# Start and end of a two-layer decoder trunk: other load order, other place for the semaphore starts, a shorter last Newton chain, and a shared last scaling

## The chip, the cores and the metric

The kernel runs on one core of a Trainium2 chip. The metric is device time in microseconds (us) of one execution, as the median of several. The program is one launch; all weights and inputs are in HBM at its start, and the output is in HBM at its end.

## The reference

Two layers over x (1 x 512 x 1024, f32), with 256 memory tokens:

```python
for i in range(DEPTH):                       # DEPTH = 2
    h = rms_norm(x, attn_norm_w[i])
    proj = h @ w_in[i]                       # q, k, v, latents, xq and the gates
    y_a = (differential attention) @ w_o_diff[i]
    y_b = (latent attention) @ w_o_mla[i]
    mh = rms_norm(mem, mem_norm_w[i])
    y_c = (cross attention into mh @ w_mem_kv[i]) @ w_o_cross[i]
    x = x + (g_a * y_a + g_b * y_b + g_c * y_c) @ w_out[i]
    h2 = rms_norm(x, ffn_norm_w[i])
    f_gate, f_up = split(h2 @ w_gate_up[i])
    x = x + (silu(f_gate) * f_up) @ w_down[i]
return rms_norm(x, final_norm_w)
```

with `rms_norm(x, w) = x * rsqrt(mean(x*x) + 1e-6) * w`. The rope tables come from cos and sin of `positions`.

## The kernel before

It is written engine by engine, with semaphores by hand; each engine runs its own list in the order in which it stands, so the order of the code is the order of the work.

**Tiling.** x is kept transposed: xT has 8 tiles (`KD`) of 128 channels by 512 tokens. A weight column block of 128 (a "slot") is 8 tiles of 128 x 128. To multiply f32 at f32r speed, each operand is split in a high and a low part, and a product is three matmuls (L602 to L604, in `unit`): high by high, low by high, high by low. 512 columns are one matmul.

**A slot's way.** SyncE loads it in two DMAs into one of two `raw` buffers (L434, in `slot`), after `slot_lo` says that the buffer is free again. ScalarE copies it to `w_hi` (L1109; for the first four slots by `first_slot`, L1367). GpSimd subtracts to get `w_lo` (L564). Then TensorE may use it. There are four w_hi/w_lo pairs. `slot_lo` starts at 2 by two small memsets of GpSimd (L536).

**The start (layer 0).** x comes in four column quarters of 512 KB (`load_x`, L422; semaphores in_x0 to in_x3), laid out with tokens on the partitions. After seven small matmuls on the identity (L874), TensorE transposes x tile by tile (`flip_x`, L876 to L882, four 128 x 128 transposes a tile, two tiles a quarter) into seven PSUM banks. ScalarE turns a tile into `h_hi`, times the gain (`first_tile`, L1372), VectorE makes `h_lo` (L1977). The first two slots of layer 0, here called N0 (cross query) and N1 (a gate), are multiplied by h tile by tile; N0 waits for each h_lo tile (`tile_split`, L889). Before N0 six tiles are transposed, and tiles 6 and 7 stand between N0's second and third tile. After N1 come the transposes of the memory tokens (L910), which wait for `mem_scaled`; then six of the eight tiles of slot N2; then the column sums of squares of x (L614), which wait for `x_sum` (`sq_added`); then the rest. x_sum is built by ScalarE's squares (L1403, four of 128 x 1024) and VectorE's adds (L1989, three, and L1990). The squares stand behind the memory's squares (L1389), a copy of slot N2, an activation table load (L1394) and the memory's 1/rms (L1397, L1399). A second table, that of Sin (loaded at L1374), serves sin_t and half_t (L1385, L1386), which wait for VectorE's angles (L1960 to L1973, from `pos_i`).

**Semaphore starts.** Each engine begins with `start_counts` (L406): one semaphore increment for each counter that it drives: 9 for TensorE (L576), 35 for VectorE (L1639) and 37 for ScalarE (L1106).

**The end.** The last tile of the down projection is done in two halves of 256 tokens (`last_down`, L1052). Behind each half VectorE adds it to xT (L2215), makes the gained copy (L2218), ScalarE squares (L1622), VectorE adds into x_sum (L2220), TensorE transposes (L1073) and sums over the channels (L1083, result `ssq`), ScalarE takes Ln and Exp (L1626, L1628), VectorE refines in `newton` (four operations, L1781 to L1784, 128 x 2). Then each half has two blocks of 128 tokens by 1024 to scale and store: the even one by VectorE (L2225), stored by SyncE (L521), and the odd one by ScalarE (L1631), stored from ScalarE's queue (L1633).

## Time and profile before

| | |
|---|---|
| median of 3 runs | 1964.63 us (1964.38 to 1966.5) |
| the profiled execution, its own time | 1964.07 us |
| its span, first to last instruction | 1961.9 us |
| TensorE busy | 1947.8 us (99%) |
| VectorE, ScalarE, GpSimd busy | 1037.2, 935.8, 1074.4 us |
| the chain that ended last | TensorE 98%, GpSimd 1% |
| TensorE's mean granted clock | 0.999 |

"Busy" adds up the time in which an engine had an instruction under way. The chain that ended last is followed back from the last instruction, at each step to whatever released it. A kernel whose chain is TensorE at 98% can gain without fewer matmuls only where TensorE stands idle: here 14.1 us of the span.

### The profile page before, as it was taken

How to read it: one execution, taken by the hardware profiler on the slowest of the kernel's cores; microseconds unless marked ns; L12 is line 12 of the kernel's file. 1: busy time of each engine (PE TensorE's matmuls, PEld its weight loads, DVE VectorE, ACT ScalarE, POOL GpSimd, SP SyncE). 2: the span in 40 equal slices, each digit the busy share in tenths (PEclk: the TensorE clock that was granted, in tenths of full speed). 3: DMA queues.
4: the chain of work that ended last, by engine and by line, in shares of the span. 5: the costliest groups of instructions: out<-in, count | busy, mean ns of one | idle time of the engine just before them, and what ended most of it. 6: DMA issues, size and time to landing. Idle time of an engine off the chain costs nothing.

```text
span 1961.9 us, 28882 instructions
## 1 busy us (share of the span) xinstructions
PE 1947.8 (99%) x9340; PEld 1632.6 (83%) x9340; DVE 1037.2 (53%) x1900; ACT 935.8 (48%) x1665; POOL 1074.4 (55%) x1422
## 2 busy tenths in 40 slices
PE   8999999999999999999999999999999999999998
PEld 7888888888888888888888888888888888888887
DVE  6445888887655333321144658888876443333111
ACT  6444666776544322233344456776674342222332
POOL 6654454445554555557765645344445555555674
PEclk9999999999999999999999999999999999999999
DMA  6443233224543333333344323223356333333232
GB/s 195 128 148 92 76 91 87 81 76 140 183 145 96 102 95 98 94 115 89 109 138 120 111 85 92 81 76 89 90 158 191 113 99 94 98 96 96 84 92 91
DMA packets 356001, 212.61 MB, mean 108 GB/s; under 512 B 14274, under 2 KB 339906, under 8 KB 355396
## 3 DMA queue, kind: packets, MB, share of 16 engines
q1 hardware_dynamic: 338288, 173.32, 30.7%
q10 hardware_dynamic: 17620, 38.07, 5.5%
q8 instruction: 56, 0.92, 0.2%
q14 instruction: 37, 0.30, 0.0%
HBM read 190.88 MB, written 20.45 MB: 108 GB/s over the span
## 4 chain that ended last, share of the span: by engine, by line
PE 98%; POOL 1%; DVE 0%; issue 0%; DMA 0%; ACT 0%; SPq 0%; POOLq 0%
PE proj L602 24%; PE proj L604 24%; PE proj L603 24%; PE score L602 2%; PE score L603 2%; PE score L604 2%; PE flip L656 2%; PE score L638 2%; PE score L816 1%; PE score L818 1%; PE score L642 1%; PE score L641 1%; PE att L583 1%; PE att L584 1%; PE att L582 1%; PE score L830 1%
## 5 line engine op out<-in xcount | busy, mean ns | idle before, releaser
L564 POOL TENSOR_TENSOR w_lo<-raw,w_hi 128x256 fp32r<-128x256 f32 x1376 | 1069.3, 809 | 866.1 <-ACT w_hi L1109 864.9
L602 PE MATMUL proj<-h_hi,w_hi 128*128 128x512 f32 x1584 | 626.3, 395 | 0.6 <-DVE h_lo L1977 0.3
L604 PE MATMUL proj<-h_hi,w_lo 128*128 128x512 f32 x1584 | 618.1, 390 | 0.0
L603 PE MATMUL proj<-h_lo,w_hi 128*128 128x512 f32 x1584 | 616.9, 389 | 0.0
L1109 ACT ACTIVATE w_hi<-raw 128x1024 fp32r<-128x1024 f32 x344 | 362.5, 1055 | 195.4 <-PE proj L604 55.2
L604 PEld LDWEIGHTS proj<-h_hi,w_lo 128*128 128x128 f32 x1584 | 297.3, 188 | 63.3
L602 PEld LDWEIGHTS proj<-h_hi,w_hi 128*128 128x128 f32 x1584 | 297.6, 188 | 60.6 <-issue 0.9
L603 PEld LDWEIGHTS proj<-h_lo,w_hi 128*128 128x128 f32 x1584 | 297.7, 188 | 58.9 <-issue 0.2
L602 PE MATMUL proj<-hid_hi,w_hi 128*128 128x512 f32 x330 | 129.0, 391 | 0.0
L604 PE MATMUL proj<-hid_hi,w_lo 128*128 128x512 f32 x330 | 128.5, 389 | 0.0
L603 PE MATMUL proj<-hid_lo,w_hi 128*128 128x512 f32 x330 | 128.4, 389 | 0.0
L1580 ACT ACTIVATE sig_f<-gate_n 128x512 f32<-128x512 f32 x44 | 27.8, 632 | 163.1 <-DVE gate_n L2176 163.1
L1109 ACT ACTIVATE hid_hi<-hid 128x512 f32 (+1 forms) x44 | 27.8, 633 | 160.8 <-DVE hid L2183 160.8
L2176 DVE TENSOR_TENSOR gate_n<-proj,rstd 128x512 f32<-128x512 f32 x44 | 30.3, 688 | 129.7 <-PE proj L604 129.7
L1109 ACT ACTIVATE pt_hi<-flip 128x384 fp32r<-128x384 f32 (+1 forms) x112 | 55.4, 532 | 89.1 <-PE flip L656 88.8
L1722 DVE TENSOR_TENSOR pt_lo<-flip,pt_hi 128x384 fp32r<-128x384 f32 (+1 forms) x112 | 64.7, 607 | 62.1 <-ACT pt_hi L1109 62.1
L2183 DVE TENSOR_TENSOR hid<-proj,gated 128x512 f32<-128x512 f32 x44 | 30.4, 691 | 106.1 <-PE proj L604 106.0
L1942 DVE TENSOR_TENSOR xT<-xT,proj 128x512 f32 x24 | 16.5, 687 | 120.3 <-PE proj L604 120.3
L604 PEld LDWEIGHTS proj<-hid_hi,w_lo 128*128 128x128 f32 x330 | 61.9, 188 | 12.9
L603 PEld LDWEIGHTS proj<-hid_lo,w_hi 128*128 128x128 f32 x330 | 62.0, 188 | 12.7
L602 PEld LDWEIGHTS proj<-hid_hi,w_hi 128*128 128x128 f32 x330 | 62.0, 188 | 12.7
L602 PE MATMUL score<-outs_hi,w_hi 128*128 128x512 f32 x160 | 62.3, 390 | 0.0
(420 smaller groups left out, 3147.2 us busy)
## 6 DMA issues: line engine op xcount, KB each, us to landing
raw<-in_w_in SPq DMA_DIRECT2D x224, 256.0 KB, 3.1
raw<-in_w_gate_up SPq DMA_DIRECT2D x176, 256.0 KB, 3.0
raw<-in_w_down SPq DMA_DIRECT2D x96, 192.0 KB, 2.5
gate_in<-gate_scratch ACTq DMA_DIRECT2D x48, 256.0 KB, 4.1
gate_scratch<-gate_out ACTq DMA_DIRECT2D x46, 256.0 KB, 2.0
raw<-in_w_mem_kv SPq DMA_DIRECT2D x32, 256.0 KB, 2.9
raw<-in_w_o_diff SPq DMA_DIRECT2D x32, 256.0 KB, 2.9
raw<-in_w_out SPq DMA_DIRECT2D x32, 256.0 KB, 2.9
```

What stands on the lines that cost most here:

```text
L564: ins = g.tensor_tensor(w_lo[s][:, cols], raw[s % 2][:, cols], w_hi[s][:, cols].bitcast(F32), ALU.subtract)
L582: mm(o, sh, mh, start=n == 0, stop=False)
L602: mm(o, hi[:, c:c + width], rh, start=start and k == 0, stop=False)
L603: mm(o, hi[:, c:c + width], rl, start=False, stop=False)
L604: ins = mm(o, lo[:, c:c + width], rh, start=False, stop=stop and k == n - 1)
L638: ins = mm(o, mqT[0:96, cols], mkT[0:96, 0:(t + 1) * P], start=t != 0, stop=t == group[-1])
L656: ins = nc.tensor.transpose(b[:, col:col + P], p[:, q_off(t) + j * P:q_off(t) + (j + 1) * P], ident[:, :])
L1109: return sc.activation(out, in_, ACT.Copy)
L1580: sc.activation(sig_f[:, e, :], gate_n[:, :], ACT.Sigmoid).then_inc(silu_sig.sem, 1)
L1722: v.tensor_tensor(dst, src, hi.bitcast(F32), ALU.subtract).then_inc(flip_read.sem, 1)
L2176: v.tensor_tensor(gate_n[:, :], proj[0][:, :], rstd[:, :], ALU.mult).then_inc(gate_read.sem, 1)
L2183: v.tensor_tensor(hid[:, e, :], proj[1][:, :], gated[:, :], ALU.mult).then_inc(hid_ready.sem, 1)
```

## The change

Seven edits, six of them in the start and the end:

- SyncE: slot N0's weights are loaded first, then quarters 0 and 1 of x, slot N1's weights, quarters 2 and 3, the memory.
- TensorE: the transposes of tiles 4, 5 stand before N0's third tile and those of 6, 7 before its fifth; four tiles are transposed ahead of N0.
- ScalarE's 37 semaphore starts are issued by TensorE, behind its seven small matmuls. ScalarE issues the DMA of the positions before that of the gains.
- ScalarE takes the two Sin behind its second tile of h, and its copy of slot N2 behind the memory's 1/rms.
- Last norm: VectorE forms w0 = -(ssq + eps)/2 when ssq has been read by Ln (beside Exp), and then r*r, times w0, and (that + 1.5) * r: three operations behind Exp, where four were.
- The last odd block: ScalarE scales 768 columns, VectorE 256, ahead of its own even block.
- ScalarE's store waits for VectorE's counter too, SyncE's second store for its third count, TensorE's last sums for `half_shifted` where they waited for `y_rstd`.

```diff
+SHARE = 768
@@ sync
-            load_x(0)
-
                 slot(l, "N", 0, 0, *whole(w_in, l, C_XQ))
                 if l == 0:
-                    for quarter in range(1, 4):
-                        load_x(quarter)
+                    load_x(0)
+                    load_x(1)
                 slot(l, "N", 0, 1, *gate(l, GATES_N))
                 if l == 0:
+                    load_x(2)
+                    load_x(3)
                     sp.dma_start(mem_in[:, :, :], mem[0, :, :].rearrange("(t p) d -> p t d", p=P)).then_inc(in_mem, 16)
@@
-                sp.wait_ge(y_scaled[0], n + 1)
+                sp.wait_ge(y_scaled[0], 2 * n + 1)
@@ tensor
+            start_counts(pe, "act")
@@
-            for k in range(KD - 2):
+            for k in range(KD // 2):
                 flip_x(k)
@@
-                    if l == 0 and k == 2:
-                        flip_x(KD - 2)
-                        flip_x(KD - 1)
+                    if l == 0 and k in (2, 4):
+                        flip_x(k + 2)
+                        flip_x(k + 3)
@@
                 if half:
-                    pe.wait_ge(y_rstd, 1)
+                    pe.wait_ge(ssq_read.sem, ssq_read.end(DEPTH) + 1)
+                    pe.wait_ge(half_shifted, 1)
@@ scalar
+            act.dma_start(pos_i[:, :], positions[:, :]).then_inc(in_pos, 16)
             act.dma_start(gains[:, 0:GAIN_COLS], gain_cols[:, :]).then_inc(in_gain, 16)
-            act.dma_start(pos_i[:, :], positions[:, :]).then_inc(in_pos, 16)
             act.wait_ge(const_ready, 1)
-            start_counts(act, "act")
@@
                 first_tile(k)
+                if k == 1:
+                    act.wait_ge(pre_vec, 1)
+                    sc.activation(sin_t[:, :, :], ang[:, :, :], ACT.Sin)
+                    sc.activation(half_t[:, :, :], ang[:, :, :], ACT.Sin, scale=0.5).then_inc(pre_act, 1)
@@
-            act.wait_ge(pre_vec, 1)
-            sc.activation(sin_t[:, :, :], ang[:, :, :], ACT.Sin)
-            sc.activation(half_t[:, :, :], ang[:, :, :], ACT.Sin, scale=0.5).then_inc(pre_act, 1)
@@
-            first_slot(2)
             act.dma_start(lam_in...)
             sc.preload_act_table_set(LN_EXP)
...
             sc.activation(mem_rstd[:, :], mem_rstd[:, :], ACT.Exp, scale=-0.5).then_inc(pre_act, 1)
+            first_slot(2)
@@
-                sc.activation(y_out[:, t, :], y_out[:, t, :], ACT.Copy, scale=rstd[:, t:t + 1]).then_inc(y_scaled[1], 1)
+                c = SHARE if half else D
+                sc.activation(y_out[:, t, 0:c], y_out[:, t, 0:c], ACT.Copy, scale=rstd[:, t:t + 1]).then_inc(y_scaled[1], 1)
                 act.wait_ge(y_scaled[1], half + 1)
+                act.wait_ge(y_scaled[0], half + 1)
@@ vector
+                part = slice(t, t + 2)
+                ve.wait_ge(ssq_read.sem, ssq_read.end(DEPTH) + half + 1)
+                v.tensor_scalar(newton_w[:, 0:2], ssq[:, part], EPS, -0.5, ALU.add, ALU.mult).then_inc(half_shifted, 1)
+                ve.wait_ge(half_shifted, half + 1)
                 ve.wait_ge(rms_ready.sem, rms_ready.end(DEPTH) + half + 1)
-                newton(rstd, t, 2).then_inc(y_rstd, 1)
+                chain(v.tensor_tensor(newton_w[:, 2:4], rstd[:, part], rstd[:, part], ALU.mult))
+                chain(v.tensor_tensor(newton_w[:, 2:4], newton_w[:, 2:4], newton_w[:, 0:2], ALU.mult))
+                v.scalar_tensor_tensor(rstd[:, part], newton_w[:, 2:4], 1.5, rstd[:, part], ALU.add, ALU.mult).then_inc(y_rstd, 1)
                 ve.wait_ge(y_rstd, half + 1)
                 ve.wait_ge(y_copied, KD + half)
+                if half:
+                    v.tensor_scalar(y_out[:, 3, SHARE:D], y_out[:, 3, SHARE:D], rstd[:, 3:4], None, ALU.mult).then_inc(y_scaled[0], 1)
                 v.tensor_scalar(y_out[:, t, :], y_out[:, t, :], rstd[:, t:t + 1], None, ALU.mult).then_inc(y_scaled[0], 1)
```

The first instructions of SyncE, the engine whose queue loads everything (raw_60 and raw_61 are the two raw buffers; the lines are those of the kernel that each stands in):

```order
-L422 DMA x_in<-in_x 128x4x256
-L434 DMA raw_60<-in_w_in 128x4x128 x2
-L422 DMA x_in<-in_x 128x4x256 x3
-L434 DMA raw_61<-in_w_in 128x4x128 x2
-L470 DMA mem_in<-in_mem 128x2x1024
+L434 DMA raw_60<-in_w_in 128x4x128 x2
+L424 DMA x_in<-in_x 128x4x256 x2
+L434 DMA raw_61<-in_w_in 128x4x128 x2
+L424 DMA x_in<-in_x 128x4x256 x2
+L472 DMA mem_in<-in_mem 128x2x1024
```

N0's weights now come ahead of x's first quarter, N1's ahead of the third.

TensorE at N0, before (flip, att, score, proj are PSUM banks that the transposes of x go to; a unit's matmuls go to proj):

```order
L881 MATMUL proj<-ident,x_in 128x128 x4
L602 MATMUL proj<-h_hi,w_hi_62 128x512
L603 MATMUL proj<-h_lo,w_hi_62 128x512
L604 MATMUL proj<-h_hi,w_lo_66 128x512
L602 MATMUL proj<-h_hi,w_hi_62 128x512
L603 MATMUL proj<-h_lo,w_hi_62 128x512
L604 MATMUL proj<-h_hi,w_lo_66 128x512
L881 MATMUL score<-ident,x_in 128x128 x4
L881 MATMUL flip<-ident,x_in 128x128 x4
```

and in the change:

```order
L884 MATMUL score<-ident,x_in 128x128 x4
L604 MATMUL proj<-h_hi,w_hi_62 128x512
L605 MATMUL proj<-h_lo,w_hi_62 128x512
L606 MATMUL proj<-h_hi,w_lo_66 128x512
L604 MATMUL proj<-h_hi,w_hi_62 128x512
L605 MATMUL proj<-h_lo,w_hi_62 128x512
L606 MATMUL proj<-h_hi,w_lo_66 128x512
L884 MATMUL score<-ident,x_in 128x128 x4
L884 MATMUL proj<-ident,x_in 128x128 x4
```

Two tiles (8 transposes) have moved from ahead of N0 to behind its second tile, and the last two from there to behind its fourth.

ScalarE between the copy of x's tile 4 and its squares, before:

```order
L1385 ACTIVATE sin_t<-ang 128x96
L1386 ACTIVATE half_t<-ang 128x96
L1389 ACTIVATE mem_sq,mem_ss<-mem_in 128x1024 x2
L1109 ACTIVATE w_hi_64<-raw_60 128x1024
L1392 DMA lam_in<-in_diff_lambda 128x512
L1394 ACT_TABLE_LOAD
L1397 ACTIVATE mem_rstd<-mem_ss,eps 128x2
L1399 ACTIVATE mem_rstd<-mem_rstd 128x2
L1403 ACTIVATE x_sq<-xT 128x1024
```

and in the change:

```order
L1393 ACTIVATE mem_sq,mem_ss<-mem_in 128x1024 x2
L1395 DMA lam_in<-in_diff_lambda 128x512
L1397 ACT_TABLE_LOAD
L1400 ACTIVATE mem_rstd<-mem_ss,eps 128x2
L1402 ACTIVATE mem_rstd<-mem_rstd 128x2
L1112 ACTIVATE w_hi_64<-raw_60 128x1024
L1407 ACTIVATE x_sq<-xT 128x1024
```

The two Sin have left this stretch for an earlier one, and the copy of slot N2 stands behind the memory's 1/rms.

## Rows read from the trace of the kernel before

**Rows 1.** Two windows, TensorE alone: window, length, busy (instructions), granted clock, DMA share, GB/s.

```profile
0.00:45.00 45.00, 38.29 (x210) 1.00 0.61 191
45.00:200.00 155.00, 155.00 (x833) 1.00 0.41 123
```

**Rows 2.** Timeline of TensorE, 0 to 32: start, length, what [idle before <- releaser].

```profile
2.19 3.16 PE L874 MATMUL proj<-ident 128*128 128x128 f32 x14 [2.19 <-POOL pool_mark L541]
5.18 1.04 PE L881 MATMUL flip<-ident,x_in 128*128 128x128 f32 x8
8.09 0.66 PE L881 MATMUL att<-ident,x_in 128*128 128x128 f32 x4 [1.86 <-DMA x_in<-in_x]
10.80 0.50 PE L602 MATMUL proj<-h_hi,w_hi 128*128 128x512 f32 x1 [0.27 <-POOL w_lo L564]
17.95 0.39 PE L602 MATMUL score<-h_hi,w_hi 128*128 128x512 f32 x1
18.18 0.40 PE L603 MATMUL score<-h_lo,w_hi 128*128 128x512 f32 x1
...
31.42 1.12 PE L614 MATMUL score<-x_sum,ones 128*128 128x512 f32 x2 [1.51 <-DVE x_sum L1990]
```

**Rows 3.** Timeline of ScalarE, 0 to 10.

```profile
1.25 0.53 ACTq L1104 DMA_DIRECT2D pos_i<-in_positions  x1
4.68 1.28 ACT L1374 ACT_TABLE_LOAD   x1 [4.68 <-issue]
6.81 1.06 ACT L1109 ACTIVATE w_hi<-raw 128x1024 fp32r<-128x1024 f32 x1 [0.63 <-DMA raw<-in_w_in]
```

**Rows 4.** DMA to landing (us): x's quarters (L422), N0's weights (L434), gains and positions.

```profile
DMA to landing us min/median/max: 4.0/6.1/7.2
```
```profile
DMA to landing us min/median/max: 4.4/4.6/4.9
```
```profile
gains<-in_gain_cols ACTq DMA_DIRECT2D x1, 36.0 KB, 3.3
pos_i<-in_positions ACTq DMA_DIRECT2D x1, 2.0 KB, 4.1
```

**Rows 5.** Timeline of GpSimd, 4 to 11.

```profile
6.38 0.12 POOL L556 MEMSET pool_mark<- 128x1 f32 x1
7.95 2.79 POOL L564 TENSOR_TENSOR w_lo<-raw,w_hi 128x256 fp32r<-128x256 f32 x4 [1.45 <-ACT w_hi L1109]
```

**Rows 6.** Timeline of ScalarE, 15 to 28.

```profile
15.26 0.69 ACT L1372 ACTIVATE h_hi<-flip,gains 128x512 fp32r<-128x512 f32 x1
...
16.31 0.31 ACT L1385 ACTIVATE sin_t<-ang 128x96 f32<-128x96 f32 x1
...
23.23 1.06 ACT L1109 ACTIVATE w_hi<-raw 128x1024 fp32r<-128x1024 f32 x1 [0.62 <-DMA raw<-in_w_mem_kv]
...
24.19 2.94 ACT L1403 ACTIVATE x_sq<-xT 128x1024 f32<-128x1024 f32 x3
```

**Rows 7.** Timeline of VectorE, 8 to 32.

```profile
9.82 0.74 DVE L1977 SCALAR_TENSOR_TENSOR h_lo<-flip,gains,h_hi 128x512 fp32r<-128x512 f32 x1
...
25.26 4.97 DVE L1989 TENSOR_TENSOR x_sq<-x_sq 128x1024 f32<-128x1024 f32 x3 [1.56 <-ACT x_sq L1403]
30.27 1.10 DVE L1990 TENSOR_TENSOR x_sum<-x_sq 128x512 f32<-128x512 f32 x1
```

**Rows 8.** The chain that ended last, 1956 to the end: start, length, what.

```profile
1956.06 0.17 DVE square L1781
...
1956.84 1.15 ACT y_out L1631
```

**Rows 9.** Timeline of the end: the scalings and the stores.

```profile
1956.85 0.75 DVE L2225 TENSOR_SCALAR y_out<-y_out,rstd 128x1024 f32<-128x1024 f32 x1
1957.63 0.36 SPq L521 DMA_DIRECT2D out<-y_out  x1
1958.02 0.34 ACTq L1633 DMA_DIRECT2D out<-y_out  x1
```

**Rows 10.** A window of the end: busy of PE, PEld, DVE, ACT, POOL, granted clock, DMA share, GB/s.

```profile
1959.00:1960.00 1.00, 0.00 (x0) 0.00 (x0) 0.00 (x0) 0.00 (x0) 0.00 (x0) 0.50 1.02 418
```

More of the change, by code:

```diff
@@ L167, in build_trunk @@
         lam_scale = here("lam_scale", [P, NT])
+        newton_w = here("newton_w", [P, NT])
         rstd_n, rstd_n2, kv_mean, kv_scale = (here(n, [P, NT]) for n in ("rstd_n", "rstd_n2", "kv_mean", "kv_scale"))
@@ L363, in build_trunk @@
         x_moved, x_gate, x_squared, mem_copied = (sem(n) for n in ("x_moved", "x_gate", "x_squared", "mem_copied"))
-        half_done, half_added, half_squared, half_summed = (sem(n) for n in ("half_done", "half_added", "half_squared", "half_summed"))
+        half_done, half_added, half_squared, half_summed, half_shifted = (sem(n) for n in ("half_done", "half_added", "half_squared", "half_summed", "half_shifted"))
         rope_flipped, rope_read = sem("rope_flipped"), sem("rope_read")
```

## The prediction

> **What bounds the kernel now.** I read the windows of TensorE first, since it is busy for 99% of the span. From 45 us to 1940 us it is busy in every window to the last digit, of which the first stands for all nine [rows 1]; so whatever is saved at the start arrives at the end unchanged, and nothing in between is touched. Its idle time is 6.7 us in the first 45 (45.00 - 38.29) [rows 1], and the other 7.4 of the 14.1 in the table fall behind 1940. The change works on these 14 us alone, and could not save all of them. About what a measurement of this kernel tells from no change is 0.2%, or 3.9 us.
>
> Then the timeline of TensorE at the start [rows 2]. It waits four times: for its first work until 2.2, for x's second quarter 1.86, for the first w_lo 0.27 ahead of N0 (its busy rows hide more of that wait, since ends of matmuls are modelled), and 1.51 for x_sum, until 31.42. The last is the one to look at: x_sum comes from a chain on ScalarE and VectorE, not from TensorE, so TensorE's own earlier start is worth only as much as x_sum moves. From 31.42 on TensorE never waits again before the tail.
>
> **Start, the first load.** ScalarE's first copy (w_hi of N0) begins at 6.81, released by the DMA of the weights [rows 3]: the second of its two DMAs was issued at 1.75 and took 4.9 [rows 4]. x's first quarter, issued at 0.75, landed 4.0 later, at 4.75. With the two exchanged, the weights land at about 4.9 and the quarter at about 6.7. The gains take the place of the positions on the other queue, which landed 4.1 after 1.25, at 5.35 [rows 3, 4]; the copy waits for them too. So w_hi begins at about 5.4 and ends at 6.45. GpSimd's memsets end at 6.50 [rows 5], so w_lo begins at 6.55 where it began at 7.95: 1.4 earlier, and it ends at 9.35. Bounds: 0.8 (gains late by 0.6) to 1.45 (nothing but GpSimd's memsets).
>
> **Start, the 37 semaphore starts.** On ScalarE they fill the time from the end of the positions' issue, 1.78, to the table load at 4.68 [rows 3]: 2.90 us, 78 ns each. Off ScalarE they give nothing by themselves: the table load then ends near 3.1, but the copy waits for data until 5.4. On TensorE they stand behind seven matmuls that run from 2.19 to 5.35 [rows 2] and ahead of the first transposes, which now can't begin before 6.7. If TensorE's queue hands out increments while matmuls are under way, they cost nothing; if they begin only when the last one has started, they end at 5.1 + 2.9 = 8.0, and the transposes are 1.3 late. No row shows which. I take nothing, since 1.35 of the 2.9 lie in the wait for x anyway and the rest has 3.2 us of matmuls to hide in; the other end is priced below. The Trainium skill (Advanced Engine Details and Errata, Engine Queue Depths) gives TensorE a queue of 64 entries, against 8 for ScalarE; by that the increments run ahead, cost nothing, and the sum stays 1962.8, where a queue that holds them back gives 1963.8. No row here shows a queue's depth.
>
> **Start, tile by tile.** With durations of the same operations (eight transposes 1.0 at most, with 0.11 to 0.13 from one to the next; three matmuls 0.69, at 0.23 each [rows 2]; h_hi 0.69 long and 0.6 apart [rows 6]; h_lo 0.74 long [rows 7]): tiles 0, 1 are transposed from 6.8 to 7.75, tiles 2, 3 from 8.1 (the second quarter's landing is what it was, [rows 2]) to 9.1. h_lo of tile 0 is ready at 8.8, so w_lo decides: N0 begins at 9.4, not 10.80, its second tile at 10.1. Then stand two tiles of transposes; x's third quarter now lands behind N1's weights, where the fourth did, 3.59 + 7.2 = 10.8 [rows 4], just when TensorE comes to it. They end at 11.75, N0's third and fourth tiles at 13.15, tiles 6, 7 at 14.05 (the last quarter lands at 12.5), and the last four tiles at 16.8. TensorE's total is the same 7.2 us of matmuls and transposes; N1 begins at about 16.8 against 17.7 [rows 2].
>
> **Start, x_sum.** ScalarE's last h_hi ends at 14.9 instead of 15.9, since its transposes end earlier (0.95 saved). The two Sin (0.35 up to the next start [rows 6]) move to 8.6, behind h_hi of tile 1, where they delay tile 2's h_hi to 9.6; N0 takes it at 11.75, so the cover is over a us. The move of the copy of N2 past the table load saves the memory's scaling 1.0 and costs the squares nothing; TensorE then finds the memory scaled at 21.5, needed at 22.3. Between the first square and the next three stands the copy of slot N3, at which ScalarE waited 0.62 for a DMA [rows 6]; that DMA is issued once w_lo of N1 is done, now at 14.0 instead of 16.6, so this wait goes. Together 0.95 + 0.35 + 0.6 = 1.9, less 0.1 for the memory landing no earlier than it did: the three squares begin at 22.4 instead of 24.19. VectorE's adds follow them (25.26 becomes 23.45) and take the same 6.1 us, slowed as before by GpSimd's subtraction beside them [rows 7]; x_sum is there at 29.6 instead of 31.4. TensorE comes to it at 28.15, waits 1.45, and goes on **1.8 us earlier**. What is late next: slot N2's w_lo, now begun at 20.4 instead of 19.9 and done at 23.7, needed at 23.95; and N4's weights, whose load waits for it and lands at about 27, when ScalarE comes to copy it. Both just fit.
>
> **End.** Behind the first half everything lies beside the second half's matmuls. Behind the second, four small VectorE operations begin at 1956.06 [rows 8], 0.195 apart, and the scalings at 1956.85. One goes: 0.2 saved, w0 fits beside Exp. ScalarE's 768 columns take 1.15 less 0.23 (0.9 ns a column, an estimate from the 1.06 of 1024 columns [rows 3] and the 0.6 that 512 take [rows 6]): its store is issued at 1957.6 instead of 1958.02. VectorE's 256 columns (an estimate of 0.3, between a quarter of the 0.75 of 1024 columns and half of it [rows 9]) go ahead of its own block, so SyncE's store moves from 1957.63 to 1957.75 [rows 9]. The first store is then as early as before, and the two together are one stretch of DMA at 418 GB/s, full [rows 10]: 1.05 MB in 2.5 us. The end is set by the first store's issue, not by the last one's. Saved: 1957.63 - 1957.58 = 0.05. Bounds: -0.1 (the later second store counts) to 0.3 (issue of the later one decides, 1958.02 to 1957.75).
>
> **Sum.** 1964.07 - 1.8 - 0.05 = 1962.2 for an execution like the profiled one. It stands 0.56 below the median of the runs, so by the median 1964.63 - 1.85 = **1962.8**.
>
> **Rivals.** (a) The starts delay TensorE. Transposes begin at 8.0, h_lo of tile 0 is ready at 10.0, N0 begins there, and its end is that of before, 17.8; ScalarE's last h_hi ends at 15.8, and x_sum gains only the Sin and the wait at slot N3, 0.8 in all: 1963.8. For it speaks that the same increments held ScalarE up in full [rows 3]. Chance 0.24.
>
> (b) The start does nothing: x's third and fourth quarters, now behind both slots' weights, come a us late, and ScalarE's chain ends where it did; or w_lo of N2, half a us later, takes over the wait. Against it: the order of bytes up to N1's weights is permuted, not longer. 1964.6. Chance 0.1.
>
> (c) The clock. TensorE's first matmuls run at its lower level: 14 in 3.16, 0.23 each, where transposes of that shape are 0.11 to 0.13 apart at once afterwards [rows 2]; and at the end, with TensorE idle since 1955.5, the granted clock falls to 0.50, which is 1.2 GHz [rows 10]. In the change TensorE has nothing to do from 5.35 to 6.8 and little until 9.4. If the clock falls in that stretch, each 512-column matmul at 1.2 GHz takes 0.22 more. 1.45 of it is hidden by the wait for x_sum, and 1.85 is the gain, so n slow matmuls give -1.85 + 0.22 n - 1.45: slower from n = 15; all 24 of N0 make it 1966.6, and N1 too (48) 1971.9, beyond 0.2% from n = 33. Against it: before, TensorE was idle for 1.9 at a time in the same stretch and the clock stayed. Chance 0.05, of which 0.02 beyond 0.2%. The Trainium skill (TensorE: Matmul & The Clock Gate, Part 1) has the throttled clock as the default that activity lifts, and so speaks against any wait put between the warming matmuls and N0; by that, rival (c) is the result. Of that a row here shows one side only, the fall at the end [rows 10].
>
> (d) More than forecast, up to the 1.45 that TensorE still waits and 0.3 at the end: 1961.1. Chance 0.03.
>
> **How the numbers follow.** Forecast (starts hidden) 0.58, (a) 0.24, (b) 0.10, (c) 0.05, (d) 0.03. The range takes in the forecast with the bounds of its terms, (a) and (b), and half a us for the scatter of the median, whose runs lie 2.1 apart: 1961.3 to 1965.0. Faster by over 0.2% (below 1960.7) 0.02, within 0.2% 0.96, slower by over 0.2% 0.02.
>
> **What would show it.** Right: N0's w_hi at 5.4, its w_lo at 6.55, first transposes at 6.7 to 6.8 released by x's DMA, N0 at 9.4, no wait of ScalarE ahead of slot N3's copy, the sum of squares begun at 29.6, first store issued near 1957.6 less the start's gain, and no more than 0.1 between the end's saving and zero. The starts are at fault if the transposes wait for no DMA and begin near 8. Wrong altogether if TensorE shows idle time between 45 and 1940, or N0's matmuls are 0.4 apart.

## The result, and the profile after

The changed kernel takes **1968.49 us** (median of 20 runs, 1965.96 to 1969.7), against 1964.55 (1963.72 to 1966.8) for the kernel before beside it. The ratio of the two sets of runs is 1.0017, with a 95% interval of 1.0011 to 1.0023; by the medians the change is slower by 3.9 us. The prediction was 1962.8 us, so it was wrong in sign, and the time lies outside its range.

The profiled execution took 1969.58 us, its span is 1967.8 us (before: 1961.9), so 5.9 us are to be found in it. I compared the same places on TensorE and VectorE in both traces:

| place | before | after | difference |
|---|---|---|---|
| N0's first matmul | 10.80 | 11.89 | +1.1 |
| sum of squares of x | 31.42 | 32.40 | +1.0 |
| transposes of p_a, the first layer's attention weights | 49.82 | 53.24 | +3.4 |
| second half's add to xT | 1953.50 | 1958.38 | +4.9 |
| end of the span | 1961.9 | 1967.8 | +5.9 |

So there are four pieces: 1.0 at the start, 2.4 ahead of p_a, 1.5 just behind it, 1.0 at the end. TensorE's timeline of the changed kernel shows the start (it answers to [rows 2]):

```profile
2.18 3.32 PE L876 MATMUL proj<-ident 128*128 128x128 f32 x14 [2.18 <-POOL pool_mark L543]
8.56 1.97 PE L884 MATMUL flip<-ident,x_in 128*128 128x128 f32 x8 [3.06 <-DMA x_in<-in_x]
10.33 1.06 PE L884 MATMUL att<-ident,x_in 128*128 128x128 f32 x4
11.18 1.06 PE L884 MATMUL score<-ident,x_in 128*128 128x128 f32 x4
11.89 0.78 PE L604 MATMUL proj<-h_hi,w_hi 128*128 128x512 f32 x1
12.47 0.63 PE L605 MATMUL proj<-h_lo,w_hi 128*128 128x512 f32 x1
...
32.40 1.12 PE L616 MATMUL score<-x_sum,ones 128*128 128x512 f32 x2 [0.96 <-DVE x_sum L1996]
...
53.24 1.09 PE L840 MATMUL flip<-ident,p_a 128*128 128x128 f32 x8 [2.28 <-DVE p_a L1723]
```

The eight first transposes take 1.97 us where they took 1.04 [rows 2], and the first matmuls of N0 are 0.42 to 0.58 apart instead of 0.23: TensorE works at about half speed until 13.3. What released them was x's DMA. SyncE's timeline, and the time from issue to landing of x's four quarters:

```profile
0.87 1.00 SPq L434 DMA_DIRECT2D raw<-in_w_in  x2
1.92 1.05 SPq L424 DMA_DIRECT2D x_in<-in_x  x2
```
```profile
DMA to landing us min/median/max: 6.6/7.1/8.4
```

The first quarter, issued at 1.92, landed 6.6 later, at 8.5; in front of the weights it had landed after 4.0 [rows 4].

The wait ahead of p_a, on the engines that feed it, first in the kernel before:

```profile
43.34 1.06 ACT L1109 ACTIVATE w_hi<-raw 128x1024 fp32r<-128x1024 f32 x1 [1.29 <-DMA raw<-in_w_mem_kv]
...
46.55 1.69 DVE L1717 TENSOR_SCALAR p_a<-p_a,inv_m 128x256 f32<-128x256 f32 x4
...
49.82 1.04 PE L838 MATMUL flip<-ident,p_a 128*128 128x128 f32 x8
```

and in the change:

```profile
42.44 1.59 SPq L434 DMA_DIRECT2D raw<-in_w_mem_kv  x2
...
46.84 1.06 ACT L1112 ACTIVATE w_hi<-raw 128x1024 fp32r<-128x1024 f32 x1 [3.79 <-DMA raw<-in_w_mem_kv]
...
47.90 0.46 ACT L1152 ACTIVATE p_a<-score,bias_m 128x256 f32<-128x256 f32 x1
47.98 5.79 POOL L566 TENSOR_TENSOR w_lo<-raw,w_hi 128x256 fp32r<-128x256 f32 x8 [2.71 <-ACT w_hi L1112]
...
50.06 3.12 DVE L1723 TENSOR_SCALAR p_a<-p_a,inv_m 128x256 f32<-128x256 f32 x4
```

The load is issued at 42.44 instead of 39.59, the copy comes at 46.84 instead of 43.34, the four exponentials queue behind it, and VectorE's normalisations of p_a (the division by the row sums) take 3.12 instead of 1.69, beside eight subtractions of GpSimd in a row. Behind the wait, windows of TensorE (busy, granted clock, DMA share, GB/s in the columns that end each row):

```profile
54.00:56.00 2.00, 2.00 (x14) 0.59 0.39 114
56.00:58.00 2.00, 2.00 (x12) 0.55 0.56 166
58.00:60.00 2.00, 2.00 (x13) 1.00 0.00 0
```

From 54.3 to 57.7 matmuls of 256 columns are 0.21 apart, where they were 0.12: the granted clock is near 0.5, its lower level of 1.2 GHz, after TensorE stood idle from 50.97 to 53.24. That is the third of the pieces, 1.5 us.

The end, to be held beside [rows 8, 9]:

```profile
1961.01 0.16 DVE L2232 TENSOR_TENSOR newton_w<-rstd 128x2 f32<-128x2 f32 x1
...
1961.59 0.94 ACT L1636 ACTIVATE y_out<-y_out,rstd 128x768 f32<-128x768 f32 x1 [0.69 <-DVE rstd L2234]
1961.59 0.35 DVE L2238 TENSOR_SCALAR y_out<-y_out,rstd 128x256 f32<-128x256 f32 x1
1961.86 0.75 DVE L2239 TENSOR_SCALAR y_out<-y_out,rstd 128x1024 f32<-128x1024 f32 x1
1962.56 0.36 ACTq L1639 DMA_DIRECT2D out<-y_out  x1
...
1962.64 0.36 SPq L523 DMA_DIRECT2D out<-y_out  x1
```

The arithmetic is as forecast: the scalings begin 3.21 after the second half's add (3.35 before), and the first store is issued 4.18 after it (4.13). But the last of the two lands 8.96 after the add, 8.0 before.

### The profile page after: what moved, and what is told of

Read it like the earlier page. It is cut to its first block, busy times and chain, and to the rows that moved or that the text cites. A ratio compares the mean times of both kernels' runs of the same rounds, so it can differ in the third digit from the quotient of the medians.

```text
span 1967.8 us, 28888 instructions
## 1 busy us (share of the span) xinstructions
PE 1950.9 (99%) x9340; PEld 1636.4 (83%) x9340; DVE 1041.0 (53%) x1901; ACT 936.8 (48%) x1665; POOL 1076.8 (55%) x1422
## 4 chain that ended last, share of the span: by engine, by line
PE 97%; POOL 1%; issue 1%; DVE 0%; DMA 0%; ACT 0%; DVEq 0%; ACTq 0%; SPq 0%; POOLq 0%
PE proj L604 24%; PE proj L606 24%; PE proj L605 24%; PE score L604 2%; PE score L606 2%; PE score L605 2%; PE flip L658 2%; PE score L640 2%; PE score L820 1%; PE score L818 1%; PE score L644 1%; PE score L643 1%; POOL w_lo L566 1%; PE att L585 1%; PE att L586 1%
```

## The experiments

Eighteen kernels, each timed in eleven runs, beside 21 to 33 runs of the kernel before on the same chip. An interval of a single ratio is 0.09% wide to either side, 1.8 us; so no verdict hangs on one median, but on medians that repeat and on what each profile shows. Differences below are to the before of the same batch.

### Which part of the change: four kernels

Undo the moved copy, `first_slot(2)`, in the change; move it alone in the kernel before; undo the whole end (Newton part and shared scaling) in the change; make the new end alone.

```diff
@@ e1: the change;  e2: the kernel before, the other way round
+            first_slot(2)
             act.dma_start(lam_in...)
...
-            first_slot(2)
             act.wait_ge(x_gate, 1)
```

> The change, with one move undone: ScalarE copies slot N2 ahead of the activation table load again, as before. Theory S (the moved copy): in the changed kernel this copy came at 22.5 instead of 18.7, GpSimd subtracted slots N2, N3, N4 back to back until 35.8 instead of 33.3, the slot loads behind them came up to 3.8 us late, ScalarE stood at a slot's DMA ahead of the exponentials until 46.8, and TensorE waited 2.3 us for the probabilities at its transposes of p_a and then ran 3.5 us at half clock (1.5 us lost). With the move undone that wait is gone or under 0.5 and the clock stays: 3 to 4 us faster than the change, 1964.5 to 1965.5. Theory L (the load order alone, everything behind it is shifted by it): the wait at p_a stays over 1.5 and the time stays within 1 us of the change, 1967.5 to 1969.

> The kernel before, with only the copy of slot N2 moved behind the memory's 1/rms. Theory S: GpSimd's subtraction of N2 starts about 2.8 us later than in the kernel before; the probabilities there had 1.6 us to spare, so TensorE now waits 0.5 to 2 us for p_a, with up to 1.5 more if its clock falls: slower than before by 0.5 to 3.5 us. Theory L: the move is hidden and the time is that of the kernel before, within 0.5 us.

> The change, with the end undone (four Newton steps, ScalarE scales all 1024 columns); the start is that of the change. From the second half's last sum on, the kernel before took 8.4 us to the end and the changed one 9.4, though its first store was issued 0.1 nearer to that point. Theory E (the new end makes the stores worse): 0.8 to 1 us faster than the change. Theory N (the longer landing of the stores comes from something else, such as instruction fetches that fall beside them, or is scatter): within 0.4 us of the change, slower by 0.1 if anything.

> The kernel before, with only the new end. Theory E: 0.8 to 1 us slower than before. Theory N: between 0.3 faster and 0.1 slower than before, and the stores land 2.5 to 3.5 us after their issue as before.

| | median | before | ratio (95%) | wait for p_a |
|---|---|---|---|---|
| e1, copy back | 1965.46 | 1964.36 | 1.0004 (0.9995 to 1.0013) | none |
| e2, copy alone | 1963.96 | 1964.36 | 0.9998 (0.9989 to 1.0007) | 1.2 |
| e3, end undone | 1967.45 | 1964.36 | 1.0014 (1.0005 to 1.0023) | 2.2 |
| e4, end alone | 1965.43 | 1964.36 | 1.0008 (0.9999 to 1.0017) | none |

The change stood 3.9 above its before; with the copy undone it is 1.1, with the end undone 3.1, so the copy is worth 2.8 and the end 0.85; the new end alone costs 1.07. But the copy alone costs nothing that the medians show: it needs something else of the change beside it. And the start, which was to give 1.8, gives nothing.

The profiles say more on the start, if the places at which TensorE reads x_sum are put side by side. In the eight kernels whose start is that of before (before, e4 to e10) it is 31.42 to 33.40, since x's second quarter lands later in one run than in another (the third tile's transposes begin anywhere from 8.09 to 9.97). So the +1.0 of the first table is within that scatter. With the copy moved and the loads as before (e2, e11, e15, e18, some of them described below) it is 30.23 to 31.12, earlier than in all eight; with the copy moved and the new load order (the change, e3, e14, e17) 31.83 to 32.41. The moved copy does bring x_sum forward, and the late first quarter of x takes it back.

### The end: what costs a microsecond

All kernels with the new end showed landings of 3.8 and 4.7 us for stores issued 0.08 apart, the others 2.6 and 3.5 for stores 0.4 apart. My first theory was that distance.

The stretch from the second half's add to the end of the span repeats to 0.05 us or better from profile to profile, much closer than any median: 8.38 to 8.39 before and in e2, e3, 9.39 in the change, e1 and e4. The new end costs 1.0 there.

```diff
@@ e7, own block first (e8 stores both blocks from SyncE, ScalarE's first)
-                if half:
-                    v.tensor_scalar(y_out[:, 3, SHARE:D], ...).then_inc(y_scaled[0], 1)
                 v.tensor_scalar(y_out[:, t, :], ...).then_inc(y_scaled[0], 1)
+                if half:
+                    v.tensor_scalar(y_out[:, 3, SHARE:D], ...).then_inc(y_scaled[0], 1)
```

> Theory Q (the new end costs 1 us because its two last stores are issued within 0.1 us of each other on two queues; then a tail of the data, with one DMA engine in sixteen at work, lasts 1 us longer): with the shorter Newton part alone the stores stay 0.4 apart (SyncE's first), so the landings stay at 2.6 and 3.5 us and the time is that of before less the operation saved, -0.2 us. Theory N (the Newton part itself costs it, w0 beside Exp delaying it): +0.5 to +1.0 us.

> The shared scaling alone, with four Newton steps. Theory Q: stores within 0.15 us of each other, landings 3.8 and 4.7 us, and the time +1.2 us to before (the whole of the new end's +1.0, and the 0.2 that the Newton part saves). Theory N: stores land as in before and the time is within 0.3 us of before.

> The new end with VectorE's own block first and its 256 columns of ScalarE's block behind it: SyncE's store is issued 0.2 us earlier than in before, ScalarE's some 0.35 us after it. Theory Q: landings 2.6 to 2.8 and 3.5 us, no tail of the data, time -0.2 to -0.4 us to before. If it is the splitting of a block between two engines, or the ScalarE queue's later wait, and not the distance of the stores: +1.0 us as with the change's order.

> The new end with both blocks of a half stored from SyncE's queue, ScalarE's block first; the second issue follows the first by its own length, 0.36 us. Theory Q in the form 'two queues at once': no tail, the last landing 3.5 us after the second issue, time 0 to +0.2 us to before. In the form 'two transfers that wait side by side, on whatever queue': the tail stays, +1.0 us.

Measured, against 1964.51: e5 1964.23, e6 1964.40, e7 1965.03, e8 1964.90 (intervals from 0.9989 to 1.0013). **The theory fell.** In e6 the stores are 0.08 apart and land after 3.4 and 3.8 without a tail; in e7 they are 0.32 apart and have one (landings up to 4.5). From the add to the end of the span e5 takes 8.25 us, e6 8.56, e7 9.22 and e8 9.37: each half of the new end is nearly harmless, both together are not, in whatever order. What differs shows in the DMA view of the last microseconds; e4, 1957 to 1963:

```profile
DMA packets 289, 1.06 MB, mean 176 GB/s; under 512 B 32, under 2 KB 32, under 8 KB 288
...
q1 hardware_dynamic: 144, 0.52, 21.7%
q10 hardware_dynamic: 144, 0.52, 21.6%
q14 instruction: 1, 0.01, 0.3%
...
out<-y_out ACTq DMA_DIRECT2D x1, 512.0 KB, 3.8
out<-y_out SPq DMA_DIRECT2D x1, 512.0 KB, 4.7
```

One packet more, of another queue: 8 KB of **instructions**. It took 309 ns, 1.9 us into the stream of the stores; behind it the stream has a tail, in which one packet after the other of a single DMA engine's share is left. Windows of e4 (the last two columns are DMA share and GB/s):

```profile
1961.00:1961.25 0.25, 0.00 (x0) 0.00 (x0) 0.00 (x0) 0.00 (x0) 0.00 (x0) 0.50 0.73 295
1961.25:1961.50 0.25, 0.00 (x0) 0.00 (x0) 0.00 (x0) 0.00 (x0) 0.00 (x0) 0.50 0.10 17
1961.50:1961.75 0.25, 0.00 (x0) 0.00 (x0) 0.00 (x0) 0.00 (x0) 0.00 (x0) 0.50 0.08 33
1961.75:1962.00 0.25, 0.00 (x0) 0.00 (x0) 0.00 (x0) 0.00 (x0) 0.00 (x0) 0.50 0.04 16
1962.00:1962.25 0.25, 0.00 (x0) 0.00 (x0) 0.00 (x0) 0.00 (x0) 0.00 (x0) 0.50 0.04 16
```

A share of 0.06 is one engine in sixteen. In the kernel before, the share falls from 0.88 to 0.03 between one quarter of a us and the next. In kernels without a tail the same packet comes 1.8 to 2.4 us after the last landing. Counting the built lists explained who has it: VectorE's is 2076 instructions long before (also e2, e3), 2077 in e6, 2078 in e5, and 2079 in the change and in e1, e4, e7, e8, all those with a tail. Two kernels test it, one each way:

```diff
@@ e9: the kernel before, three instructions more (six waits long met, two to an instruction)
+            for _ in range(3):
+                ve.wait_ge(x_moved, 1)
+                ve.wait_ge(pre_vec, 1)
             for half in range(2):
@@ e10: the new end alone (e4), one instruction less
-                ve.wait_ge(y_flipped, KD - 2)
+                if not half:
+                    ve.wait_ge(y_flipped, KD - 2)
```

> The kernel before with three more instructions in VectorE's list (waits that have long been met, in its idle time ahead of the last halves), and nothing else: 2079 instructions, as many as every kernel so far whose stores had a tail, where those without one had 2076 to 2078. Theory F (the length of VectorE's list decides when an 8 KB packet of instructions is fetched; with 2079 it falls into the stream of the last stores and holds up one DMA engine): a tail, landings of the last stores up by 0.8 to 0.9 us, the packet within 2.2 us of the stream's start, time +0.7 to +1.0 us to before. Theory X (the tail comes from the shared block or the Newton part itself): no tail, 0 us.

> The kernel before with the whole new end, less one wait of VectorE that is met already (the second half's for y_flipped): 2078 instructions, otherwise the kernel that took 1.07 us more than before. Theory F: no tail, the last landing by 3.4 and 3.8 us after the issues as with the sharing alone, time -0.1 to -0.3 us to before. Theory X: tail, +1.0 us.

Measured, against 1964.22: e9 **1965.03**, +0.8 (ratio 1.0004, 0.9995 to 1.0013); e10 **1963.93**, -0.3 (0.9997, 0.9988 to 1.0006). The DMA view of the end of e9 (from 1957), and under it that of e10, in which no instruction queue appears at all:

```profile
q14 instruction: 1, 0.01, 0.3%
...
out<-y_out SPq DMA_DIRECT2D x1, 512.0 KB, 3.6
out<-y_out ACTq DMA_DIRECT2D x1, 512.0 KB, 4.4
```
```profile
DMA packets 288, 1.05 MB, mean 210 GB/s; under 512 B 32, under 2 KB 32, under 8 KB 288
...
out<-y_out ACTq DMA_DIRECT2D x1, 512.0 KB, 3.4
out<-y_out SPq DMA_DIRECT2D x1, 512.0 KB, 3.8
```

Three instructions that do nothing, in a kernel otherwise untouched, bring the packet and the tail; one instruction less in the new end takes both away. The stretch from the add to the end is 9.34 us in e9 against 8.38, and 8.43 in e10 against 9.39 in e4: the tail costs 0.96 either way. This part is shown. The medians alone would not have done: e9's interval takes in 1. Why a packet of 0.31 us makes the stream of the stores 0.85 longer (3.49 us in e4, 2.64 in e10) is open. In all twenty profiles of the study the tail is there with 2079 instructions (ten kernels) and absent with 2076 to 2078 (ten). The Trainium skill (Trainium Kernel Development and Optimization, Key Constraints) has the DMAs issued from the queues of SyncE, ScalarE and GpSimd run on the same 16 engines and interleave. For the two store queues these rows agree (144 packets of each, with an equal share); that the instruction packets share the engines as well is what the tail shows here.

### Ahead of p_a, and the start

```diff
@@ e11: loads and first transposes as before;  e14: starts back on ScalarE;  e15: both;  e13: starts on TensorE alone
-            start_counts(pe, "act")
+            start_counts(act, "act")
@@ e12: the copy back (e1) and one wait less (e10)
@@ e17: the change, and on ScalarE, where its starts had stood
+            for _ in range(37):
+                act.sem_inc(spare, 1)
```

> The change with its loads and its first transposes in the order of before; the moved copy of slot N2, the semaphore starts on TensorE, the Sin, the positions and the new end stay. Theory L (x's first quarter behind the weights is what makes the start late, and the late start is what lets the moved copy stop TensorE at p_a): the quarter lands 4 us after its issue, N0 begins before 10.9, the wait for p_a is at most 1.2 us and the granted clock stays at 1.00, time 2.5 to 3.5 us below the change. Rival T (the semaphore starts on TensorE, or the other edits of ScalarE, make the start late): N0 begins at 11.5 or later, the wait for p_a stays at 2 us or more, within 1 us of the change.

> The change with the copy of slot N2 back ahead of the table load, and with one wait of VectorE less (2078 instructions). If the two causes are all there is (S: the moved copy given the late start, 3.0 us; F: the fetch in the last stores, 0.9 us), they add: 1968.5 - 3.0 - 0.9 - 0.1 = 1964.5, within 0.5 us of before. If F is wrong it is 1965.5, as with the copy back alone.

> The kernel before with ScalarE's 37 semaphore starts issued by TensorE, and nothing else. Theory P (TensorE issues them in order, 64 ns each, 2.35 us in all, behind the warming matmuls, and the idle time drops its clock): transposes begin near 7.9 where x has landed at 4.8, the first eight take 1.9 us instead of 1.0, N0 begins at 12 or later instead of 10.8; the wait for x_sum (1.5 us) hides part of it, time +0.3 to +1.5 us to before. Rival H (they are hidden, and the 2.35 us in the kernel with the loads back had another cause): transposes at 5.2, N0 at 10.8, 0 us.

> The change with the 37 starts on ScalarE again; its load order stays. Theory W (two causes side by side: the starts hold TensorE until 7.9 and x's late quarter until 8.5, so that taking away one leaves the other): transposes begin within 0.6 us of 8.5 released by x's DMA, still at half speed, the wait for p_a still near 2 us; time within 1 us of the change. Theory P alone (the starts are the cause): N0 before 11, no wait for p_a over 1.2 us, time 2.5 to 3.5 us below the change.

> The change with both undone: starts on ScalarE, loads and transposes as before; the moved copy of N2, the early Sin and the new end stay. Theory W: transposes at 5.2 at full speed, N0 at 10.8, wait for p_a at most 1.2 us, clock at 1.00; what is left over before is the fetch in the last stores, +1.0, less 0.1 to 0.3: 1965.0. If the moved copy, or the early Sin, costs by itself: wait for p_a of 2 us and 1967 or more.

> The change with 37 increments of an unused semaphore on ScalarE, where its starts stood before; TensorE keeps the starts, loads, copy and end stay. TensorE's start is then as late as in the change, and ScalarE has the list and the timing of the kernel with the starts back (1965.2). Theory G (what moved is on ScalarE: 37 instructions fewer put its fetch of an 8 KB packet of instructions at 39 us, between the loads that the copies ahead of p_a wait for, instead of at 13 us): packet at 13 us, no wait for p_a over 1.2 us, 1965 to 1966. Theory P (it is TensorE's idle time and its clock): wait for p_a of 1.9 to 2.3 us, 1967.5 to 1969.

| | median | before | first transposes | tail | wait for p_a |
|---|---|---|---|---|---|
| e11, loads back | 1966.34 | 1964.22 | 7.86, half speed | yes | 1.9 |
| e12, copy back, one wait less | 1964.79 | 1964.22 | 7.96, half speed | no | none |
| e13, starts alone | 1964.18 | 1964.40 | 7.86, half speed from 9.2 | no | none |
| e14, starts back | 1965.22 | 1964.40 | 8.63, half speed | yes | none |
| e15, starts and loads back | 1965.19 | 1964.40 | 5.30, half speed | yes | none |
| e17, ScalarE padded | 1968.07 | 1964.39 | 8.50, half speed | yes | 2.2 |

**The starts do hold TensorE.** The first transposes of e11, with x landed at 4.75:

```profile
7.86 1.94 PE L884 MATMUL flip<-ident,x_in 128*128 128x128 f32 x8 [2.35 <-issue]
```

TensorE's warming matmuls end at 5.51; 2.35 us of "issue" for 37 increments are 64 ns each. e13 has the same start and wait (7.86, 2.35). But alone they cost nothing in the median, -0.2, where I had expected 0.3 to 1.5: N0 begins at 11.63 instead of 10.80, but the small waits behind it (0.35 for h_lo, 0.28 for the memory) are gone, and TensorE comes to x_sum at 29.98 instead of 29.91. In the change they lie beside the late quarter of x and are not seen; in e3, in whose run the quarter landed sooner, the transposes begin at the same 7.86.

**The wait for p_a needs two edits together**, the copy moved and the starts on TensorE: without the one (e1, e12) or the other (e14, e15) it is gone, and the medians are 0.6 to 1.1 above before. The new load order adds to it: e11, without it, keeps 1.9 of the 2.3 and is 2.1 above before, which fits neither theory L (N0 before 10.9, at most 1.2; it was 12.87) nor rival T (within 1 us of the change). No run has the two edits and nothing else. e12, which undoes the copy and the tail, is 0.6 above before where at most 0.5 was expected, within its interval. Taking away the starts removed the wait although x landed as late as in the change. That went against my theory P, which had promised it only with N0 before 11, and against W, which expected the wait to stay. e17 then settled which engine: with ScalarE's list and timing restored but the starts left on TensorE the wait is 2.2 and the time that of the change. Theory G fell.

What the starts change on TensorE besides its start is where its own packets of instructions (16 KB) come. The last pair of loads before p_a, and the nearest such packet:

| | pair issued | TensorE's packet (decimals cut off) | both issues took | issue to copy | wait for p_a |
|---|---|---|---|---|---|
| before | 39.59 | 42.8 | 0.94 | 3.75 | 0 |
| e1 | 40.97 | 44.1 | 0.93 | 3.74 | 0 |
| e14 | 41.87 | 45.0 | 0.93 | 3.58 | 0 |
| e18 | 40.73 | 43.8 | 0.93 | 3.64 | 0 |
| change | 42.44 | 42.4 | 1.59 | 4.40 | 2.28 |
| e3 | 42.13 | 42.0 | 1.70 | 4.33 | 2.2 |
| e11 | 40.55 | 40.5 | 1.33 | 4.11 | 1.9 |
| e17 | 42.49 | 42.5 | 1.43 | 4.28 | 2.2 |
| e2 | 39.57 | 42.3 | 0.93 | 5.38 | 1.2 |

In all four kernels with a wait of 1.9 or more the packet comes within 0.15 us of the issue of the pair, and the two issues take 1.3 to 1.7 us instead of 0.93. In e2 it meets the end of the load, whose last packets straggle as those of the stores did. In e18 a later pair, issued at 43.70 with the packet at 43.8, takes 1.52 us and hurts nobody. This is no peculiarity of the place: of all pairs of weight loads in the twenty traces from 12 us on, the 91 issued within 0.2 us of a 16 KB packet took 1.10 to 1.92 us (median 1.38), the 6538 with none within 0.95 us at most 1.28 (median 0.93). The trace of the kernel before has three of the 91, at 64.24, 1026.57 and 1472.21, of 1.19, 1.64 and 1.38 us. SyncE's timeline of e18, and its DMA view from 43.7 to 43.9:

```profile
40.73 0.93 SPq L436 DMA_DIRECT2D raw<-in_w_mem_kv  x2
43.70 1.52 SPq L436 DMA_DIRECT2D raw<-in_w_in  x2
```
```profile
q8 instruction: 1, 0.02, 30.0%
```

The lateness of 0.4 to 0.8 that this gives is then added to: in e14 the copy comes at 45.45 and the normalisations take 1.67, since GpSimd's four subtractions end at 49.41, in their midst; in the change the copy comes 1.39 later and they take 3.12. The twenty profiles divide here without an exception. In the five with a wait for p_a (the change, e2, e3, e11, e17) ScalarE's next copy follows the exponentials at once, GpSimd subtracts eight tiles in a row, and the normalisations take 2.64 to 3.17; in the other fifteen that copy waits for its own load and they take 1.67 to 1.70. So 1.4 us of the change's wait of 2.28 come from there. That a packet of TensorE at one pair or the other decides this is **argued, not shown**: no run moved TensorE's packets and nothing else. The moved copy is what puts the pair at 42.44 in the first place: GpSimd's subtractions for N2, N3 and N4 then stand back to back until 35.8, and each buffer comes free later (loads at 33.12 and 35.97 instead of 29.34 and 33.50).

### Looking for a kernel that beats both

```diff
@@ e16: the kernel before, with the new end less one wait, positions first, Sin behind the second tile
@@ e18: the kernel before, with the new end less one wait and the copy of N2 moved
```

> What of the change the runs have not spoken against, on the kernel before: the new end with one wait of VectorE less (2078 instructions), the positions first and the Sin behind ScalarE's second tile. By the terms: the end -0.3 (as measured with 2078 instructions), the Sin 0.35 off ScalarE's chain to x_sum, seen at the wait for x_sum (1.5 to 1.15 us): 1963.6 in a batch whose before is 1964.3, faster than both kernels. If the Sin's place is worth nothing: 1964.0.

> The kernel before with the two parts that cost nothing or gained in runs of their own: the copy of slot N2 behind the table load (-0.4 us alone) and the new end with VectorE at 2078 instructions (-0.3 us). If they add: 0.7 us below before, 1963.6 where before is 1964.3, faster than both kernels. If the copy's gain was scatter: -0.3 us. If the copy stops TensorE at p_a in the median (1.2 us in its profile): +0.5 us or more.

e16: 1965.25 against 1964.40 (1.0006, 0.9996 to 1.0015), not the gain forecast. In its profile x's second quarter landed so late that the third tile's transposes began at 9.28 instead of 8.09, the fifth and sixth tiles' and N0's first three matmuls ran at half speed, and x_sum was waited for until 32.57. Scatter of the DMA is enough for that: in e5, whose start is that of before, the third tile began at 9.97 and x_sum was waited for until 33.40. Why the median did not fall is open. e18: **1963.80** against 1964.39, the lowest difference of the study, -0.6, but the ratio is 1.0000 with 0.9991 to 1.0009: it beats the change clearly, the kernel before not measurably.

## Why the prediction was wrong, step by step

- **The first load.** "With the two exchanged, the weights land at about 4.9 and the quarter at about 6.7": the first half was right (w_hi at 5.43, forecast 5.4; w_lo at 6.68, forecast 6.55), the second wrong by 1.8 us. I had moved the landing by one place in the queue, but the quarter then took 6.6 instead of 4.0: time to landing belongs to what is already under way, not to the transfer. [Rows 4] had said so, with 4.0 for the first quarter and 7.2 for the last. Even with one order it varies: in the profiles with the change's loads the first transposes begin at 7.86 to 8.63.
- **The semaphore starts.** "I take nothing": wrong as to the mechanism. They are issued in order behind the matmuls, as rival (a) had it, 64 ns each; e13 shows the 2.35 us. Its price of 1.0 for the whole was not seen, since small waits (alone, e13) or x's late quarter (in the change) cover it. The Trainium skill (Advanced Engine Details and Errata, Engine Queue Depths) gives TensorE a queue of 64 entries, from which I had worked out that the increments run ahead at no cost; the 2.35 us of e13 do not agree with that use of it.
- **x_sum 1.8 earlier** became 1.0 later in the profile. The term that failed is ScalarE's last h_hi, 0.95 earlier in the sum: with transposes begun at 8.56 instead of 6.8, and at half speed, it ended at 18.2, forecast 14.9, and 2.3 later than before. The other two terms held: the three squares begin 1.2 later, so the early Sin and the wait at slot N3 that went gave 1.1, forecast 0.95.
- **The clock.** What rival (c), at 0.05, describes was there twice: on 16 transposes and the first matmuls of N0, and for 3.4 us behind p_a. Against it I had set that TensorE was idle for 1.9 at a time before, and the clock stayed; here half speed followed on 3.06 us without work in one place and 2.28 in the other. But that the idle time did it is not shown. In nine kernels (e2 is one) the transposes follow the warming matmuls without a gap and are as slow; in e13, after 2.35 us without work, the first twelve run at full speed and the next at half:

```profile
5.30 1.91 PE L881 MATMUL flip<-ident,x_in 128*128 128x128 f32 x8
```
```profile
7.86 1.06 PE L882 MATMUL flip<-ident,x_in 128*128 128x128 f32 x8 [2.35 <-issue]
```

Behind p_a the clock fell in the change and in e17, not in e3 after a wait of 2.25: from p_a's transposes to the second half's add it is 1905.1 to 1905.2 us in those two, 1903.7 to 1903.8 before and in e2, e3 and e11. What decides the level is open. The Trainium skill (TensorE: Matmul & The Clock Gate, Part 1) has the throttled clock as the default that activity lifts; the stretch behind p_a in the change agrees, with 0.21 us from one 256-column matmul to the next instead of 0.12, and e3 shows that such a wait need not bring it.
- **"Both just fit."** The copy of N2 was costed at nothing because TensorE had no wait left after 31.42. The chain does not end there: the delayed subtractions push later loads, the last of which ScalarE waits for in front of p_a's exponentials. By the medians this is the largest term, 2.8 us, with whatever the clock has in it. I had followed the moved work to its next user only.
- **The end, -0.05.** Newton part, lengths and issue times came as forecast, within 0.1. Without a tail the new end takes 8.43 us behind the add (e10, e12, e16, e18), that of before 8.38: +0.05 instead of -0.05, inside the bounds, and the -0.3 of e10's median is scatter. What was missing is the 0.96 of a packet of instructions, for which the sum had no term.
- **A reading.** TensorE does not wait four times in the first 45 us, but seven: waits of 0.25 for x's third quarter, 0.35 for h_lo and 0.28 for the memory make up the 0.88 that the four leave of the 6.7.
- **The sum.** 1.0 for the end (e4, and the profiles), 2.8 for the wait at p_a (e1, by medians), and nothing for the start, together 3.8; measured 3.9. e12, which undoes both, is 0.6 above before, within its interval. The chance of 0.96 for "within 0.2%" was right only by a hair: the ratio is 1.0017, and its interval reaches 1.0023.

## What to carry to other kernels

A piece of work that is moved in a queue must be followed through every buffer that it frees, until one of them is no longer waited for; a wait of 1.3 us on an engine off the critical path is a sign of how little is spare. In front of a bound engine, neither a load's time to landing nor an idle stretch of TensorE keeps its length or its clock when the order changes, nor always from one run to the next; a difference of 1 us there in one profile each says little. When an edit costs a microsecond that none of its instructions show, count the instructions of each engine and look for packets of instructions in the DMA view: one dummy instruction more or less is a cheap test. And look for a stretch that repeats: from the second half's add to the end, single profiles told 0.05 us where eleven runs told 1.8.

## What the hardware showed that I had not expected

- A fetch of 8 KB of instructions, 309 ns long, in the middle of 1 MB of stores lengthens the end by 0.96 us (e4 against e10, e9 against before), and 2079 instructions instead of 2078 on VectorE decide it in this kernel.
- A pair of DMA issues by SyncE takes 0.93 us, and 1.1 to 1.9 us when a 16 KB packet of TensorE comes within 0.2 us (91 of 91 cases).
- Semaphore increments without any wait cost 64 ns each on TensorE (2.35 us for 37) and 78 ns on ScalarE [rows 3].
- The granted clock of a window does not always tell: in the change it reads 1.00 from 8 to 14 while transposes are 0.22 apart; in e14, with the same spacing, the windows from 8 to 12 read

```profile
8.00:10.00 2.00, 1.37 (x7) 0.67 1.14 366
10.00:12.00 2.00, 2.00 (x12) 0.50 1.09 378
```

The distance from one instruction to the next is the safer sign of the clock.
- At the start of a program TensorE's level is not given by the code: eight transposes behind the same seven matmuls took 1.04 us in one profile, 1.16 and 1.30 in two and 1.77 to 1.92 in nine.
